# Two transformer blocks on one core: the sums of squares behind two norms as 32-column products, the inverse root on 128x128 values, and a third unit's products spread among them

## The chip, the cores and the metric

One core of a Trainium2 chip runs the whole program. The metric is the device time of one execution in microseconds (us), the median of several runs.

The engines are called by the names of the profile: PE (TensorE, matrix products; PEld is its weight load), DVE (VectorE), ACT (ScalarE), POOL (GpSimd) and SP (SyncE, which issues the weight loads from memory here).

## The reference, cut to what matters

The reference is two transformer blocks on a sequence of 512 tokens with 1024 features. Only a piece of it is touched by the change: twice, a sublayer's output `h` is normed and added to the residual `x`, and the new `x` is normed at once for the next sublayer.

```python
x = x + rmsnorm(h, norm_cross_post[l])               # after the cross attention
h = conv_glu_ffn(rmsnorm(x, norm_ffn_pre[l]), ...)   # first place
x = x + rmsnorm(h, norm_ffn_post[l])                 # after the gated feed-forward
qa, ... = _split(_rmsnorm(x, norm_g) @ w_in, ...)    # second place (second block)

def rmsnorm(x, gain):
    y = x * lax.rsqrt(jnp.mean(x * x, axis=-1, keepdims=True) + RMS_EPS)
    return y * gain
```

The inverse root is one number per token, so a product with the weights can be made before it is known and scaled afterwards.

## The kernel before, in words

**Data.** Activations lie feature-major: eight blocks of 128 features (partitions) by 512 tokens. Weights come as units of 128x1024 values, that is eight 128x128 pieces, one per feature block. Each unit goes through a ring of four slots: SP loads it (L536 to L543), ACT rounds it into a high part (`raise_to`, L1497), POOL subtracts to get the low part (`lower`, L552) and counts `unit_split`. PE then makes three products of 512 columns for each of the eight pieces (high by high, high by low, low by high), 24 in a unit, and counts `unit_done`. DVE reads the finished bank, scales it and counts `emptied`. A slot is loaded again when its unit is done. Every engine works its list in the order in which it is written; PE's waits sit in that list.

**The norm with the work around it.** At both places the DVE function `normed_twice` (L2128) runs over the eight blocks: it scales `h`, adds it to `x`, and makes the low part `xl` of the normed block. ACT's `prepare` (L1500) makes the high part `xh` and the square of each block (L1520, L1527). PE's `early_units` (L679) works beside them. Call the first unit of the next sublayer n0. For each block PE makes four products of n0 and n0+1 with `xh` (L701, L702), then `low_product` of the block before: the sum of squares (`token_sums`, L736) and two products with `xl` (L692). After the eighth block it makes all 24 products of n0+2 and the 24 of n0+3 (`piece`, L617). Between the second and third pieces of n0+2 it calls `spread_tokens` (L755).

**The sum and the inverse root.** `token_sums` takes the squares as the stationary operand and four columns of constants as the moving one, so that 128x4 sums come out, one per token, with tokens on the partitions. After the eighth block ACT takes the root of 128x4 values (L1511), DVE the reciprocal (L2118), and `spread_tokens` turns four columns back into a row of 512 tokens that is the same on every partition. DVE copies it into `rstd` (L2159). From there on DVE can scale n0 and n0+1.

**What follows.** Units n0, n0+1 and n0+2 are split before the norm begins. ACT raises n0+3 in the line after `prepare` (L1956 at the first place, L1971 at the second), so after the root. At the first place the next work is the gated feed-forward: DVE's `gated` (L2598) takes the units in pairs (gate and up), and PE's unit n0+6 goes into the bank of n0+4, so it waits until DVE has read n0+4 (L646). At the second place ACT squares n0 (L1976) before it raises n0+4.

Of the kernel before, what the change touches and what calls it, by code (L numbers as in the profile page):

```python
# [30 lines left out]
P = 128  # L31
# [63 lines left out]

RING = 4


FILL_START, FILL_LEVELS = 1, (0, 1, 2, 3, 4, 5, 6)
W_IN_P = 28  # L100
# [84 lines left out]
def build(nc, x_in, mem_in, w_in, par_in, con_in, moba_in, alibi_in, na_in, dist_in, out):  # L185
    with ExitStack() as ctx:
        def sb(name, shape, dt=F32):
            return ctx.enter_context(nc.sbuf_tensor(name, shape, dt))

        def sem(name):  # L190
            return ctx.enter_context(nc.semaphore(name))
# [33 lines left out]


        head_columns = sb("head_columns", [P, T * HEAD_ROWS])

        arena_r = nc.alloc_sbuf_tensor_at("arena_r", [P, ARENA], F32R, offset=arena_at)

# [156 lines left out]
        def early_bank(n0, n):  # L387

            return score_ps[:, n - n0 - 2, :] if n - n0 in (2, 3) else gemm_ps[:, n % 2, :]
# [63 lines left out]
        square_used = sem("square_used")  # L453
        std_ready = sem("std_ready")
        token_rstd_ready = sem("token_rstd_ready")
        rstd_spread = sem("rstd_spread")
        half_crossed = sem("half_crossed")
        spread_read = sem("spread_read")
# [110 lines left out]
        def _(pe):  # L569
# [47 lines left out]
            def piece(n, o, first, end, h, l):  # L617

                for kt in range(first, end):
                    w = slice(kt * P, (kt + 1) * P)  # L620
                    pe.matmul(o, wh[:, n % RING, w], h[:, kt, :], start=(kt == 0), stop=False)  # L621
                    pe.matmul(o, wh[:, n % RING, w], l[:, kt, :], start=False, stop=False)
                    m = pe.matmul(o, wl[:, n % RING, w], h[:, kt, :], start=False, stop=(kt == KT - 1))  # L623
                if end == KT:
                    m.then_inc(unit_done, 1)
# [53 lines left out]
            def early_units(n0, highs):  # L679


                keep_clock(2)
                pe.wait_ge(unit_split, n0 + 2)
                pe.wait_ge(emptied, n0)
                both = [(n, early_bank(n0, n)) for n in (n0, n0 + 1)]

                def low_product(kt):
                    take(square_ready)
                    token_sums(sq[:, kt % 2, :], kt == 0, kt == KT - 1).then_inc(square_used, 1)
                    pe.wait_ge(rhs_ready, blocks_split[0] + kt + 1)  # L690
                    for n, o in both:
                        m = pe.matmul(o, wh[:, n % RING, kt * P:(kt + 1) * P], xl[:, kt, :], start=False,  # L692
                                      stop=(kt == KT - 1))
                        if kt == KT - 1:
                            m.then_inc(unit_done, 1)

                for kt in range(KT):
                    w = slice(kt * P, (kt + 1) * P)
                    pe.wait_ge(high_made, highs + kt + 1)
                    for n, o in both:  # L700
                        pe.matmul(o, wh[:, n % RING, w], xh[:, kt, :], start=(kt == 0), stop=False)  # L701
                        pe.matmul(o, wl[:, n % RING, w], xh[:, kt, :], start=False, stop=False)  # L702
                    if kt:
                        low_product(kt - 1)
                low_product(KT - 1)
                blocks_split[0] += KT
                for n in (n0 + 2, n0 + 3):
                    pe.wait_ge(unit_split, n + 1)
                    piece(n, early_bank(n0, n), 0, 2, xh, xl)
                    if n == n0 + 2:  # L710
                        spread_tokens()
                    piece(n, early_bank(n0, n), 2, KT, xh, xl)

            def next_unit(n, h, l):

# [20 lines left out]
            def token_sums(squares, first, last):  # L736

                for c in range(T):
                    col = CCOL["col"] + 4 - c
                    m = pe.matmul(turn_ps[:, 0, 0:T], squares[:, c * P:(c + 1) * P], con[:, col:col + T],  # L740
                                  start=(first and c == 0), stop=(last and c == T - 1), skip_group_check=True)
                return m

            def token_norm(apart=1):

# [726 lines left out]
        def _(act):  # L1472
# [24 lines left out]
                    act.activation(wh[:, k % RING, :], raw[:, k % RING, :], ACT.Copy).then_inc(high_split, 1)  # L1497
                    raised[0] += 1

            def prepare(src, gain, h, ready=None, adds=0, tokens=False, banks={}):  # L1500


                base = taken.get(square_added, 0)
                act.activation(eps[:, 3:4], eps[:, 0:1], ACT.Sqrt)
                for b in range(KT):
                    high_and_square(src, gain, h, b, ready, base=base if adds else None, bank=banks.get(b))
                if adds:
                    taken[square_added] = base + adds
                if tokens:
                    take(square_used, 2)  # L1510
                    act.activation(token_std, turn_ps[:, 0, 0:T], ACT.Sqrt, bias=eps[:, 0:1],  # L1511
                                   scale=1.0 / D).then_inc(std_ready, 1)
                else:
                    finish_norm(rstd[:, :])
# [428 lines left out]
            def crossed(b):  # L1943
# [5 lines left out]
                else:  # L1949
# [2 lines left out]
            last = (FIRST["co"] + U_CO - 1) % 2  # L1952
            prepare(y, None, None, crossed, adds=KT - 3, tokens=True,
                    banks={KT - 2: score_ps[:, last, :], KT - 1: gemm_ps[:, last, :]})
            prepare(x, "norm_ffn_pre", xh, lambda b: take(block_ready), tokens=True)
            raise_to(FIRST["fup0"] + 3)  # L1956
            gated()

# [7 lines left out]
                    table_piece(arena[:, (23 + b) * N:(24 + b) * N], alibi_in[:, b * N:(b + 1) * N])  # L1966

            prepare(y, None, None, stored_and_loaded, adds=KT - 2, tokens=True)
            prepare(x, "attn_norm_e_2", xh, lambda b: take(block_ready), tokens=True)
            even, even_out = FIRST["even_in"], FIRST["even_out"]  # L1970
            raise_to(even + 3)  # L1971
            for b in range(5):
# [96 lines left out]
        def _(dve):  # L2069
# [58 lines left out]
            def normed_twice(post, pre):  # L2128


                inverse_tokens()
                added = taken.get(block_ready, 0)
                made = []

                def scale(b):
                    if b >= 2:
                        dve.wait_ge(block_ready, added + b - 1)
                    sent_stt(tmp[:, b % 2, :], y[:, b, :], p_(post, b), spread_rstd, ALU.mult, ALU.mult)
                    made.append(taken[dve_step])

                def accumulate(b):
                    dve.wait_ge(dve_step, made[b])
                    sent(dve.tensor_tensor(x[:, b, :], x[:, b, :], tmp[:, b % 2, :], ALU.add), block_ready)

                scale(0)
                accumulate(0)
                scale(1)
                for b in range(1, KT):
                    if b + 1 < KT:
                        scale(b + 1)  # L2150
                    accumulate(b)
                    low(x, pre, xh, xl, b - 1)
                low(x, pre, xh, xl, KT - 1)
                inverse_spread()

            def inverse_spread():

                inverse_tokens()
                done(dve.tensor_copy(rstd[:, :], spread_rstd))  # L2159
# [803 lines left out]
```

## Time and profile before

| what | value |
|---|---|
| median of 3 runs | 2170.68 us |
| the runs | 2167.75, 2170.68, 2171.09 us |
| the profiled execution, first to last instruction (its span) | 2169.7 us |
| PE busy | 2149.4 us, 99% of the span |
| DVE, POOL, ACT busy | 983.0, 893.9, 847.1 us |
| mean granted clock of PE | 0.997 of full speed |

Of the profiled execution the profile gives the span alone; what lies around it is not listed. In the timelines a line is a group of instructions on one engine: start from the span's start, duration in us, engine, line of the kernel, operation, result<-operands, shape of the (stationary and moving) operands, count, and in brackets the idle time before it with what ended it. Starts are measured; the ends of matrix products are modelled, so the pace of PE is read from start to start.

### The profile page before, as it was taken

What the parts mean: (1) busy time and instruction counts of PE and PEld (TensorE: products, weight loads), DVE (VectorE), ACT (ScalarE), POOL (GpSimd) and SP (SyncE); (2) the same over time, 40 slices, a digit from 0 to 9 for tenths busy, and PEclk for the clock granted to TensorE, in tenths of its full rate; (3) what the DMA queues carried; (4) which work ended last, traced back from release to release, by engine and by line L of the source; (5) the groups of instructions that cost most, each with busy time, mean ns of one, the idle gap of its engine ahead of it and who ended that gap; (6) DMA issues with size and microseconds to landing.
All of it is one profiled execution on the core that took longest, in us unless ns stands there. A gap on an engine that the chain in (4) does not pass through costs nothing.

```text
span 2169.7 us, 27420 instructions
## 1 busy us (share of the span) xinstructions
PE 2149.4 (99%) x10303; PEld 1731.4 (80%) x10303; DVE 983.0 (45%) x1496; ACT 847.1 (39%) x1282; POOL 893.9 (41%) x684
## 2 busy tenths in 40 slices
PE   9999999999999999999999999999999999999999
PEld 7875787788888877767888888888888878888887
DVE  5755645576626143465432231346534655313221
ACT  6435645422222243565433232444333434423221
POOL 5431254154444443213444444433343315444443
PEclk9999999999999999999999999999999999999999
DMA  4222132133322332102222222322222213222223
GB/s 175 78 68 69 57 99 78 59 102 122 106 97 97 110 113 88 50 30 69 97 97 97 97 97 97 106 81 75 78 87 78 72 44 109 97 97 97 97 97 97
DMA packets 55109, 193.24 MB, mean 89 GB/s; under 512 B 6112, under 2 KB 6368, under 8 KB 54752
## 3 DMA queue, kind: packets, MB, share of 16 engines
q1 hardware_dynamic: 50112, 180.41, 25.0%
q10 hardware_dynamic: 4896, 11.41, 1.6%
q8 instruction: 73, 1.20, 0.2%
q14 instruction: 28, 0.23, 0.0%
HBM read 189.69 MB, written 2.10 MB: 88 GB/s over the span
## 4 chain that ended last, share of the span: by engine, by line
issue 52%; POOL 29%; PE 17%; POOLq 1%; DMA 0%; DVE 0%; ACT 0%; SPq 0%; ACTq 0%
POOL wl L552 29%; PE gemm_ps L587 6%; PE gemm_ps L588 6%; PE gemm_ps L589 6%; POOLq L549 0%; POOLq L561 0%; DMA x<-x_in 0%; DVE xl L2090 0%; ACT xh L1892 0%; ACT wh L1497 0%; PE turn_ps L729 0%; DVE x L2236 0%; SPq L526 0%; ACTq L1891 0%
## 5 line engine op out<-in xcount | busy, mean ns | idle before, releaser
L552 POOL TENSOR_TENSOR wl<-raw,wh 128x512 fp32r<-128x512 f32 x678 | 890.1, 1335 | 1258.0 <-ACT wh L1497 1248.8
L1497 ACT ACTIVATE wh<-raw 128x1024 fp32r<-128x1024 f32 x339 | 358.7, 1059 | 752.7 <-DMA raw<-w_in 742.1
L587 PE MATMUL gemm_ps<-xh,wh 128*128 128x512 f32 x1176 | 465.8, 396 | 0.0
L589 PE MATMUL gemm_ps<-xh,wl 128*128 128x512 f32 x1176 | 459.0, 390 | 0.0
L588 PE MATMUL gemm_ps<-xl,wh 128*128 128x512 f32 x1176 | 458.8, 390 | 0.0
L588 PE MATMUL gemm_ps<-arena_r,wh 128*128 128x512 f32 (+1 forms) x1088 | 417.0, 383 | 0.0
L587 PE MATMUL gemm_ps<-arena_r,wh 128*128 128x512 f32 (+1 forms) x832 | 320.0, 385 | 1.2 <-POOL wl L552 0.7
L589 PE MATMUL gemm_ps<-arena_r,wl 128*128 128x512 f32 (+1 forms) x832 | 317.4, 381 | 0.0
L587 PEld LDWEIGHTS gemm_ps<-xh,wh 128*128 128x128 f32 x1176 | 221.5, 188 | 49.6 <-issue 2.3
L588 PEld LDWEIGHTS gemm_ps<-xl,wh 128*128 128x128 f32 x1176 | 221.5, 188 | 47.4 <-issue 2.2
L589 PEld LDWEIGHTS gemm_ps<-xh,wl 128*128 128x128 f32 x1176 | 221.3, 188 | 46.7
L588 PEld LDWEIGHTS gemm_ps<-arena_r,wh 128*128 128x128 f32 x1088 | 205.0, 188 | 41.2 <-issue 1.4
L2090 DVE SCALAR_TENSOR_TENSOR arena<-gemm_ps,rstd 128x512 f32<-128x512 f32 (+1 forms) x116 | 84.7, 731 | 261.9 <-PE gemm_ps L589 211.1
L2236 DVE TENSOR_TENSOR x<-x,gemm_ps 128x512 f32<-128x512 f32 x84 | 57.6, 686 | 316.8 <-PE gemm_ps L589 305.1
L587 PEld LDWEIGHTS gemm_ps<-arena_r,wh 128*128 128x128 f32 x832 | 157.0, 189 | 33.7 <-issue 2.4
L589 PEld LDWEIGHTS gemm_ps<-arena_r,wl 128*128 128x128 f32 x832 | 156.9, 189 | 30.1
L2097 DVE SCALAR_TENSOR_TENSOR tmp<-gemm_ps,rstd 128x512 f32<-128x512 f32 x64 | 44.2, 691 | 207.9 <-PE gemm_ps L589 207.9
L587 PE MATMUL gemm_ps<-y_r,wh 128*128 128x512 f32 x256 | 100.0, 391 | 0.0
L589 PE MATMUL gemm_ps<-y_r,wl 128*128 128x512 f32 x256 | 99.6, 389 | 0.0
L2586 DVE TENSOR_TENSOR arena_r<-sq,arena_r 128x512 fp32r<-128x512 f32 x64 | 93.7, 1464 | 2.2
L621 PE MATMUL gemm_ps<-xh,wh 128*128 128x512 f32 x216 | 88.5, 410 | 1.3 <-DVE xl L2308 0.5
L623 PE MATMUL gemm_ps<-xh,wl 128*128 128x512 f32 x216 | 84.6, 392 | 0.0
(429 smaller groups left out, 2548.6 us busy)
## 6 DMA issues: line engine op xcount, KB each, us to landing
raw<-w_in SPq DMA_DIRECT2D x338, 512.0 KB, 3.4
arena<-na_in ACTq DMA_DIRECT2D x14, 256.0 KB, 2.7
out<-x ACTq DMA_DIRECT2D x8, 256.0 KB, 2.9
x<-x_in SPq DMA_DIRECT2D x6, 256.0 KB, 6.5
arena<-alibi_in ACTq DMA_DIRECT2D x6, 256.0 KB, 3.5
arena<-moba_in ACTq DMA_DIRECT2D x1, 1024.0 KB, 4.8
arena<-mem_in ACTq DMA_DIRECT2D x1, 1024.0 KB, 5.6
arena<-dist_in ACTq DMA_DIRECT2D x1, 896.0 KB, 4.5
```

The source lines that it names most:

```text
L552: m = pool.tensor_tensor(wl[:, k, half], raw[:, k, half], wh[:, k, half].bitcast(F32), ALU.subtract)
L587: pe.matmul(o, wh[:, n % RING, w], h[:, kt, 0:width], start=(kt == 0), stop=False)
L588: pe.matmul(o, wh[:, n % RING, w], l[:, kt, 0:width], start=False, stop=False)
L589: last = pe.matmul(o, wl[:, n % RING, w], h[:, kt, 0:width], start=False, stop=(kt == nkt - 1))
L621: pe.matmul(o, wh[:, n % RING, w], h[:, kt, :], start=(kt == 0), stop=False)
L623: m = pe.matmul(o, wl[:, n % RING, w], h[:, kt, :], start=False, stop=(kt == KT - 1))
L1497: act.activation(wh[:, k % RING, :], raw[:, k % RING, :], ACT.Copy).then_inc(high_split, 1)
L2090: sent(dve.scalar_tensor_tensor(out=o, in0=a, scalar=scalar, in1=b, op0=op0, op1=op1), s)
L2097: done(dve.scalar_tensor_tensor(out=o, in0=a, scalar=scalar, in1=b, op0=op0, op1=op1), s)
L2236: sent(dve.tensor_tensor(x[:, e, :], x[:, e, :], bank(n0, e), ALU.add), emptied)
L2586: done(dve.tensor_tensor(l[:, b, :], sq[:, b % 2, :], h[:, b, :].bitcast(F32), ALU.subtract), rhs_ready)
```

## The change

At the two places, and only there:

- `tile_sums` takes the place of `token_sums`: 32 columns of ones are the stationary operand, the squares of 128 tokens the moving one. Four such products, one for each 128 tokens, go to partitions 0 to 31, 32 to 63, 64 to 95 and 96 to 127 of the same 128 columns.
- The third unit n0+2 follows one block behind n0 and n0+1: after `low_product` of blocks 0 to 4 PE makes the three products of n0+2 with that block. Blocks 5 and 6 come after the last sum.
- Then PE waits for the split of n0+3, calls `spread_tiles`, and makes block 7 of n0+2 and all of n0+3.
- ACT takes the root of 128x128 values and DVE the reciprocal of 128x128 values (each token's value stands on 32 partitions).
- `spread_tiles` makes four products whose stationary operand is one column of the identity, repeated 128 times, and whose moving operand is the 128x128 inverse roots.

The diff, without the new semaphore, the new buffer `tile_rstd` and the constant `TRAILING = 5`:

```diff
 low_product(kt):
-                    token_sums(sq[:, kt % 2, :], kt == 0, kt == KT - 1).then_inc(square_used, 1)
+                    tile_sums(sq[:, kt % 2, :], kt == 0, kt == KT - 1).then_inc(square_used, 1)
 early_units:
                     if kt:
                         low_product(kt - 1)
+                    if kt == 1:
+                        pe.wait_ge(unit_split, n0 + 3)
+                    if 0 < kt <= TRAILING:
+                        piece(n0 + 2, early_bank(n0, n0 + 2), kt - 1, kt, xh, xl)
                 low_product(KT - 1)
                 blocks_split[0] += KT
-                for n in (n0 + 2, n0 + 3):
-                    pe.wait_ge(unit_split, n + 1)
-                    piece(n, early_bank(n0, n), 0, 2, xh, xl)
-                    if n == n0 + 2:
-                        spread_tokens()
-                    piece(n, early_bank(n0, n), 2, KT, xh, xl)
+                piece(n0 + 2, early_bank(n0, n0 + 2), TRAILING, KT - 1, xh, xl)
+                pe.wait_ge(unit_split, n0 + 4)
+                spread_tiles()
+                piece(n0 + 2, early_bank(n0, n0 + 2), KT - 1, KT, xh, xl)
+                piece(n0 + 3, early_bank(n0, n0 + 3), 0, KT, xh, xl)
...
+            def tile_sums(squares, first, last):
+                for c in range(T):
+                    m = pe.matmul(turn_ps[c * HEAD_ROWS:(c + 1) * HEAD_ROWS, 0, 0:P], ones[:, 0:HEAD_ROWS],
+                                  squares[:, c * P:(c + 1) * P], start=first, stop=last)
+                return m
+
+            def spread_tiles():
+                take(tile_rstd_ready)
+                for c in range(T):
+                    row = ident[:, c * HEAD_ROWS:c * HEAD_ROWS + 1].broadcast_to([P, P])
+                    m = pe.matmul(spread_rstd[:, c * P:(c + 1) * P], row, tile_rstd[:, :], start=True, stop=True)
+                m.then_inc(rstd_spread, 1)
 prepare (ACT), with tiles=True at the two places:
-                if tokens:
+                if tiles:
+                    finish_norm(tile_rstd[:, :], P)
+                elif tokens:
 normed_twice (DVE):
-                inverse_spread()
+                take(std_ready)
+                done(dve.reciprocal(tile_rstd[:, :], tile_rstd[:, :]), tile_rstd_ready)
+                take(rstd_spread)
+                done(dve.tensor_copy(rstd[:, :], spread_rstd))
```

`finish_norm` (L1530) waits for all eight sums and takes the root of `turn_ps`, as `prepare` did before with four columns.

## Rows read from the trace of the kernel before

**Rows 1.** The page, part 1: busy us (share of the span) and instructions.

```profile
PE 2149.4 (99%) x10303; PEld 1731.4 (80%) x10303; DVE 983.0 (45%) x1496; ACT 847.1 (39%) x1282; POOL 893.9 (41%) x684
```

**Rows 2.** Timeline of PE, first place (start, duration, as said above).

```profile
412.48 0.95 PE L740 MATMUL turn_ps<-con,sq 128*128 128x4 f32 x8
413.29 0.70 PE L692 MATMUL gemm_ps<-xl,wh 128*128 128x512 f32 x2
413.83 0.40 PE L701 MATMUL gemm_ps<-xh,wh 128*128 128x512 f32 x1
...
427.49 0.95 PE L740 MATMUL turn_ps<-con,sq 128*128 128x4 f32 x8
...
428.86 0.40 PE L621 MATMUL score_ps<-xh,wh 128*128 128x512 f32 x1
...
430.24 0.60 PE L758 MATMUL turn_ps<-con,eps 128*128 128x128 f32 x4
```

**Rows 3.** Timeline of ACT, first place.

```profile
428.48 0.26 ACT L1511 ACTIVATE eps<-turn_ps,eps 128x4 f32<-128x4 f32 x1 [3.00 <-PE turn_ps L740]
428.64 1.05 ACT L1497 ACTIVATE wh<-raw 128x1024 fp32r<-128x1024 f32 x1
```

**Rows 4.** Timeline of POOL, first place.

```profile
429.76 2.53 POOL L552 TENSOR_TENSOR wl<-raw,wh 128x512 fp32r<-128x512 f32 x2 [24.47 <-ACT wh L1497]
```

**Rows 5.** Timeline of DVE, first place: reciprocal, copy, and the read of n0+4.

```profile
428.77 0.18 DVE L2118 RECIPROCAL eps<-eps 128x4 f32<-128x4 f32 x1 [4.19 <-ACT eps L1511]
430.95 0.69 DVE L2159 COPY rstd<-turn_ps 128x512 f32<-128x512 f32 x1 [2.00 <-PE turn_ps L758]
...
450.37 0.69 DVE L2090 SCALAR_TENSOR_TENSOR arena<-gemm_ps,rstd 128x512 f32<-128x512 f32 x1
```

**Rows 6.** Timeline of PE where unit n0+6 begins, first place.

```profile
450.89 0.39 PE L623 MATMUL gemm_ps<-xh,wl 128*128 128x512 f32 x1
451.12 0.50 PE L587 MATMUL gemm_ps<-xh,wh 128*128 128x512 f32 x1
```

**Rows 7.** Timeline of PE: 64-column products in pairs, between products of 128 columns.

```profile
258.75 0.40 PE L1035 MATMUL gemm_ps<-xh,wl 128*128 128x512 f32 x1
259.09 1.09 PE L882 MATMUL out_ps<-sq,arena 128*64 128x128 f32 x16
260.12 0.50 PE L1033 MATMUL gemm_ps<-xh,wh 128*128 128x512 f32 x1
260.45 0.40 PE L1034 MATMUL gemm_ps<-xl,wh 128*128 128x512 f32 x1
```

**Rows 8.** Timeline of PE: 4-column products on two column strips, and full-width ones.

```profile
184.99 1.03 PE L944 MATMUL turn_ps<-arena,con 128*4 128x512 f32 x4
...
406.97 1.88 PE L677 MATMUL out_ps<-con 128*128 128x512 f32 x4
```

**Rows 9.** Durations (ns) by line and by form: a wide reciprocal (DVE), a wide root (ACT).

```profile
L2114 DVE RECIPROCAL arena<-arena x1: 1745/1745/1745, 289.7 to 289.7; 128x256 f32<-128x256 f32 x1
...
L1532 ACT ACTIVATE rstd<-turn_ps,eps 128x512 f32<-128x512 f32 x3 | 2.1, 689 | 11.7 <-PE turn_ps L729 5.9 <-PE turn_ps L723 5.8
```

**Rows 10.** Timelines of ACT, POOL and PE, second place: square of n0, split of n0+4, n0+4.

```profile
807.32 0.63 ACT L1976 ACTIVATE sq<-arena 128x512 f32<-128x512 f32 x1 [2.71 <-DVE arena L2090]
...
808.98 5.04 POOL L552 TENSOR_TENSOR wl<-raw,wh 128x512 fp32r<-128x512 f32 x4 [1.76 <-ACT wh L1497]
...
815.96 0.49 PE L621 MATMUL gemm_ps<-xh,wh 128*128 128x512 f32 x1
```

**Rows 11.** Timeline of PE, before the second place: products at a lower clock.

```profile
780.94 1.11 PE L758 MATMUL turn_ps<-con,eps 128*128 128x128 f32 x4 [0.64 <-DVE eps L2118]
781.85 3.06 PE L677 MATMUL out_ps<-con 128*128 128x512 f32 x4
```

**Rows 12.** Busy us (count) of PE, PEld, DVE, ACT, POOL in a stretch; PEclk, DMA, GB/s.

```profile
780.80:784.20 3.40, 3.26 (x7) 1.92 (x8) 2.09 (x4) 0.53 (x1) 0.21 (x1) 0.50 0.01 2
```

**Rows 13.** Timeline of PE: 32-column transposes, all on the first strip.

```profile
834.09 0.60 PE L664 MATMUL turn_ps<-con,head_columns 128*32 128x128 f32 x4
```

More of the change, by code:

```diff
@@ L96 @@
 RING = 4
+TRAILING = 5
 FILL_START, FILL_LEVELS = 1, (0, 1, 2, 3, 4, 5, 6)
@@ L227, in build @@
         head_columns = sb("head_columns", [P, T * HEAD_ROWS])
+        tile_rstd = sb("tile_rstd", [P, P])
         arena_r = nc.alloc_sbuf_tensor_at("arena_r", [P, ARENA], F32R, offset=arena_at)
@@ L455, in build @@
         token_rstd_ready = sem("token_rstd_ready")
+        tile_rstd_ready = sem("tile_rstd_ready")
         rstd_spread = sem("rstd_spread")
@@ L1498, in raise_to, with prepare @@
                     raised[0] += 1
-            def prepare(src, gain, h, ready=None, adds=0, tokens=False, banks={}):
+            def prepare(src, gain, h, ready=None, adds=0, tokens=False, banks={}, tiles=False):
                 base = taken.get(square_added, 0)
@@ L1954, in _ @@
                     banks={KT - 2: score_ps[:, last, :], KT - 1: gemm_ps[:, last, :]})
-            prepare(x, "norm_ffn_pre", xh, lambda b: take(block_ready), tokens=True)
+            prepare(x, "norm_ffn_pre", xh, lambda b: take(block_ready), tiles=True)
             raise_to(FIRST["fup0"] + 3)
@@ L1968, in _ @@
             prepare(y, None, None, stored_and_loaded, adds=KT - 2, tokens=True)
-            prepare(x, "attn_norm_e_2", xh, lambda b: take(block_ready), tokens=True)
+            prepare(x, "attn_norm_e_2", xh, lambda b: take(block_ready), tiles=True)
             even, even_out = FIRST["even_in"], FIRST["even_out"]
```

## The prediction, before the change was run

> **What bounds the kernel now.** First the page's busy times: PE is busy for 99% of the span, every other engine for under half [rows 1]. So time is won or lost only where PE's own list gets shorter, or where it comes to stand. Next the timeline of PE at the first place. Products of 512 columns follow each other at 0.23 us: six of them fill the stretch from 428.86 to 430.24 [rows 2]. Between two blocks stands the sum of squares, eight records in 0.81 us, and the first product after it takes 0.08 us more than its slot (two products from 413.29 to 413.83) [rows 2]; a sum costs PE 0.89 us. From here PE never stands until the norm is done, since DVE and ACT are ahead of it. Then the timelines of the others, for what must be ready when. After the last sum, begun at 427.49, ACT takes the root at 428.48 and turns to the weights of n0+3 at 428.64 [rows 3]; POOL splits them from 429.76 to 432.29 [rows 4]. The reader is to see that this chain has cover: PE is in unit n0+2 (24 products and the spread) until about 434.8. DVE has its reciprocal at 428.95 and copies the spread root at 430.95 [rows 5]. Last, what DVE's start sets: it reads n0+4 from 450.37 to 451.06 [rows 5], and PE begins n0+6, which needs that bank, at 451.12, one slot of 0.23 us after 450.89 [rows 6]. DVE is just in time there, with 0.06 us to spare. This is the point on which I build.
>
> **The cheaper sums.** No row shows four 32-column products side by side. The nearest shows 64-column products on two strips: 16 records of 128 columns begin after the slot of 258.75 ends (258.98), the next full product begins at 260.12, and the one behind it is 0.33 us later instead of 0.23, so the group costs 1.14 plus 0.1 to 0.11, 1.25 us [rows 7]. One record of 128 columns in single file takes 0.11 us (four in 0.60, of which 0.27 is the last one's length [rows 2]); the 16 are therefore eight steps of two, 0.88 us, and 0.37 us is the way into and out of the narrow form. That two strips run together shows again with four 512-column records in 1.03 us, where full-width ones take 1.88 [rows 8]. The new sum has eight records. Four at a time they are two steps: 1.25 less six steps of 0.11, 0.59 us. Bounds: 0.26 us (the way in and out costs nothing) and 1.25 us (single file, 0.88 plus 0.37). I take 0.59, because rows 7 show both the steps and the way for the same record length. That saves 0.30 us a block, **2.4 us a place**.
>
> The Trainium skill speaks against the change here: "TensorEngine Tiling (Array Packing)", section "Tiling Modes", says that a change of tiling mode drains the engine. The trace agrees (the 0.37 us [rows 7]); by that page's factor of four alone a sum would be 0.22 us.
>
> **The third unit in between.** Its 24 products are the same as before; 15 come earlier. They cost nothing in themselves. The last sum starts later by 15 x 0.23 and earlier by seven cheaper sums: 427.49 + 3.45 - 2.1 = 428.84.
>
> **The wider root and reciprocal.** The root of 128x4 takes 0.26 us [rows 3], of 128x512 0.69 us [rows 9]; 128 columns add about 0.11. The reciprocal of 128x256 takes 1.75 us [rows 9], so half as wide about 0.9 against 0.18 [rows 5].
>
> **The wait for n0+3.** ACT's root began 0.99 us after the last sum's start, 0.29 after its last record [rows 2, 3]. The new sum's last record starts 0.25 us in, so the root begins at 428.84 + 0.54 = 429.38. The rounding of n0+3 follows 0.27 later (0.16 and the 0.11), POOL 1.12 us after that [rows 3, 4], and POOL's 2.53 us end at 433.30. PE has until then 0.59 for the sum and eight products (two of the last block, six of n0+2): it stands before the wait at 428.84 + 0.59 + 1.84 = 431.27. **It waits 2.0 us**, where before the same split lay under n0+2. The reciprocal is done at 429.38 + 0.4 + 0.9 = 430.7, under the same cover; were the wait gone, it would still be in time.
>
> Queued behind the wait are the spread, the last block of n0+2 and n0+3, and DVE waits for the spread.
>
> **The spread.** Four products that were transposes of one record each (0.11 us apart [rows 2]) become four with two records each, as the sums have. Bounds: 0.44 us, as now, and 0.99 us (eight steps and one weight load after the wait). I take 0.99, since other products of this operand type appear in pairs of records [rows 2]: 0.55 us more.
>
> **PE's sum** is -2.4 + 2.0 + 0.55, about +0.2 us a place.
>
> **DVE's sum, first place.** The copy of the root begins 0.38 us after the spread's last record (430.57 to 430.95 [rows 2, 5]): 433.30 + 0.11 + 0.77 + 0.38 = 434.56 instead of 430.95, 3.6 us late. DVE's two pairs of units before n0+4 fill 430.95 to 450.37 [rows 5], 9.7 us each, idle only for ACT's answers, which move along. So n0+4 is read at 454.67 and PE, at its place by 451.3, **waits for 3.3 us**: the place costs 3.5 us, PE's own 0.2 included. Later banks have room: a pair takes DVE 9.7 us and PE 48 products, 11.
>
> **Second place.** The square of n0 and the split of n0+4 move by the same 3.6 us: POOL's first two halves, from 808.98, end at 815.1 instead of 811.5, and PE wants them at 815.96 [rows 10]. Covered with 0.9 us left, so the place costs PE's 0.2. Were that gone too, 3.5 us would come here as well.
>
> SP's load of n0+4 starts with `unit_done` of n0, later by 1.05 us (1.35 for the last sum's start, less 0.30); PE has the wait, the spread and 27 products of n0+2 and n0+3 left before it wants that unit, over 9 us.
>
> **Sum:** 3.5 + 0.2 = +3.7 us. The profiled span is 2169.7, 1.0 below the median of 2170.68; on the median this is **2174.4 us**, +0.17%.
>
> **The rivals.**
>
> A. The sum above, 2173.4 to 2175.4 by its roundings: 0.40.
>
> B. *The stall lowers PE's clock.* Before the second place, after narrow products and an idle gap of 0.64 us, PE's granted clock is 0.50, that is 1.2 GHz instead of 2.4, from 780.80 to 784.20 [rows 11, 12]; four products take 3.06 us there instead of 1.88 [rows 8, 11]. The new stalls of 2.0 and 3.3 us are longer. Such a stretch of 3.4 us does half of its work: +1.7 us when it falls behind the wait at n0+6, 2176.1; two of them 2177.8. Against it: the same narrow sums before the first place left the clock alone (the 1.88 us [rows 8]). This rival is slower beyond what can be told apart: 0.32.
>
> C. *Four strips don't run together.* The 32-column transposes go one after another, four in 0.60 us [rows 13]. In single file a sum costs 0.9 to 1.25 us, up to 0.36 more than now: the sums' 2.4 us saved are lost at each place and DVE is later by as much, from +5.0 to +10.6 over A, 2179 to 2185. Rows 7 and 8 speak against it: 0.08.
>
> D. *The wait for n0+3 costs nothing,* because ACT reaches its weights sooner than I read: then PE saves 1.9 us at the second place, and DVE at the first is 1.6 us late instead of 3.6, 2170.3. The order of ACT's list speaks against it: 0.08.
>
> E. *The way in and out is hidden* under the products around it: a sum costs 0.26 us and both places gain 2.6 us more, 2169.2. Rows 7 speak against it: 0.12. The Trainium skill's page "TensorEngine Tiling (Array Packing)", section "Overview", gives up to four times the speed for 32 columns; no row here shows it for groups this short.
>
> **How the numbers follow.** 0.2%, 4.3 us, is about what a measurement can tell from no change. Slower: B, C and the upper part of A (0.09), 0.49. Faster needs D and E together, about 2165: 0.06 of their 0.20. Within: 0.45. The range leaves out C and most of E: 2170.0 to 2178.0.
>
> **What would show it.** In the changed profile: two starts of the four records of a sum within some 0.03 us, about 0.11 apart, and 0.6 us from the sum's start to the next full pace; idle time of PE before the spread, ended by POOL, of some 2 us at both places; DVE's copy of the root 3 to 4 us later than now, measured from the first block's products; and PE waiting some 3 us for DVE at n0+6 at the first place, nowhere at the second. No wait before the spread, or none at n0+6, makes the prediction wrong, and records of a sum 0.11 us apart one by one make it too low.

## The result and the profile after

The changed kernel takes 2174.56 us against 2170.19 for the kernel before (medians of 20 executions each, taken in turn). The ratio is 1.0023, with a 95% interval of 1.0016 to 1.0029: slower by 3.5 to 6.3 us. The forecast was 2174.4, "slower by over 0.2%" with a chance of 0.49.

The profiled execution has a span of 2171.9 us at a granted clock of 0.996. That is only 2.2 us over before's 2169.7. Two things outside the places hide part of the difference. Ahead of the first place the stretches at half clock (a granted clock of 0.50) lie differently, so that the kernel before reaches the second of the norm's eight blocks 1.3 us later (411.45 against 410.17); and the stages that the change doesn't touch are 1.2 us shorter in this execution of the changed kernel. So the places are compared by themselves, each from the first product of the norm's second block: first place to the first product of n0+6, second place to that of n0+4. Before, these stretches are 39.67 us (411.45 to 451.12) and 29.59 us (786.37 to 815.96).

First the timeline of PE in the changed kernel at the first place: a sum between two blocks, the last sum, and the spread.

```profile
410.86 0.39 PE L706 MATMUL gemm_ps<-xh,wl 128*128 128x512 f32 x1
411.18 0.43 PE L754 MATMUL turn_ps<-sq,con 128*32 128x128 f32 x8
411.54 0.73 PE L696 MATMUL gemm_ps<-xl,wh 128*128 128x512 f32 x2
412.11 0.40 PE L625 MATMUL score_ps<-xh,wh 128*128 128x512 f32 x1
...
427.27 0.43 PE L754 MATMUL turn_ps<-sq,con 128*32 128x128 f32 x8
...
431.71 1.16 PE L763 MATMUL turn_ps<-tile_rstd,con 128*128 128x128 f32 x8 [1.97 <-POOL wl L556]
432.62 0.48 PE L625 MATMUL score_ps<-xh,wh 128*128 128x512 f32 x1
```

These answer to [rows 2]. The sum begins 0.09 us after its slot (410.86 to 411.18 is 0.32, not 0.23), two full products follow it within 0.57 us (411.54 to 412.11) where 0.46 is their own time, and between its start and theirs lie 0.36 us: 0.09 + 0.36 + 0.11, 0.56 us in all, against 0.89 before. The new gap stands ahead of the spread: 1.97 us, ended by POOL.

The timelines of ACT, POOL and DVE beside it, in that order, answer to [rows 3 to 5].

```profile
427.77 0.37 ACT L1556 ACTIVATE tile_rstd<-turn_ps,eps 128x128 f32<-128x128 f32 x1 [2.33 <-PE turn_ps L754]
428.04 1.05 ACT L1519 ACTIVATE wh<-raw 128x1024 fp32r<-128x1024 f32 x1
...
429.16 2.49 POOL L556 TENSOR_TENSOR wl<-raw,wh 128x512 fp32r<-128x512 f32 x2 [26.31 <-ACT wh L1519]
...
428.17 0.95 DVE L2179 RECIPROCAL tile_rstd<-tile_rstd 128x128 f32<-128x128 f32 x1 [3.96 <-ACT tile_rstd L1556]
432.97 0.69 DVE L2181 COPY rstd<-turn_ps 128x512 f32<-128x512 f32 x1 [3.85 <-PE turn_ps L763]
...
452.09 0.69 DVE L2114 SCALAR_TENSOR_TENSOR arena<-gemm_ps,rstd 128x512 f32<-128x512 f32 x1
```

POOL ends the split of n0+3 at 431.65 and the spread begins at 431.71: that chain, not the reciprocal (done at 429.12), sets it. DVE's copy is 22.80 us behind the second block's first product (410.17), where it was 19.50: 3.3 us late. What that lateness does is seen where n0+6 begins (timeline of PE; before it stood there at once, [rows 6]).

```profile
449.49 0.39 PE L627 MATMUL gemm_ps<-xh,wl 128*128 128x512 f32 x1
452.83 0.50 PE L591 MATMUL gemm_ps<-xh,wh 128*128 128x512 f32 x1 [2.95 <-DVE arena L2114]
...
454.34 0.63 PE L591 MATMUL gemm_ps<-xh,wh 128*128 128x512 f32 x1
454.76 0.63 PE L592 MATMUL gemm_ps<-xl,wh 128*128 128x512 f32 x1
```

PE waits 2.95 us for DVE. From 454.34 products come every 0.43 us instead of 0.23. Three windows around it (columns as in [rows 12]):

```profile
449.80:452.80 3.00, 0.08 (x1) 0.00 (x0) 2.91 (x3) 0.00 (x0) 3.00 (x3) 1.00 0.50 172
454.30:457.70 3.40, 3.40 (x9) 2.64 (x8) 2.49 (x4) 1.67 (x2) 0.31 (x1) 0.50 0.00 0
457.80:461.20 3.40, 3.40 (x17) 2.82 (x16) 3.33 (x3) 0.00 (x0) 2.99 (x2) 1.00 0.00 0
```

In the middle one the granted clock is 0.50, that is 1.2 GHz, and 9 products of PE touch it, where 17 touch the next window of the same length. At the second place the spread waits as well, and nothing else does:

```profile
806.47 0.43 PE L754 MATMUL turn_ps<-sq,con 128*32 128x128 f32 x8
...
810.89 1.16 PE L763 MATMUL turn_ps<-tile_rstd,con 128*128 128x128 f32 x8 [1.96 <-POOL wl L556]
```

So the first place is 2.99 us longer (410.17 to 452.83), the second as long as before (789.22 to 818.84, 29.62), and the half clock behind n0+6 adds 1.6 us (n0+6 takes 7.18 us instead of 5.57). Together 4.6 us, against 4.4 between the medians.

### The profile page after: what moved, and what is told of

Read it like the earlier page. It is cut to its first block, busy times and chain, and to the rows that moved or that the text cites. A ratio compares the mean times of both kernels' runs of the same rounds, so it can differ in the third digit from the quotient of the medians.

```text
span 2171.9 us, 27438 instructions
## 1 busy us (share of the span) xinstructions
PE 2146.6 (99%) x10311; PEld 1720.6 (79%) x10311; DVE 986.0 (45%) x1496; ACT 846.9 (39%) x1282; POOL 892.6 (41%) x684
## 4 chain that ended last, share of the span: by engine, by line
issue 53%; POOL 29%; PE 17%; POOLq 1%; ACT 0%; DMA 0%; DVE 0%; SPq 0%; ACTq 0%
POOL wl L556 29%; PE gemm_ps L591 6%; PE gemm_ps L593 6%; PE gemm_ps L592 6%; POOLq L553 0%; POOLq L565 0%; DMA x<-x_in 0%; ACT xh L1916 0%; ACT wh L1519 0%; PE turn_ps L736 0%; DVE x L2263 0%; SPq L530 0%; ACTq L1915 0%
```

## The experiments

Ten kernels, each an edit of the changed kernel, each against the kernel before on the same chip in five rounds. The table sets beside each ratio what its profiled execution shows: how much longer (+) or shorter (-) the two places are than before, and what n0+6 itself took over 5.57 us (half clock at the wait). These are differences of PE's starts in the timelines, in us. In e4, e6 and e7 the second place holds some 1.6 us of a half-clock stretch. One execution of each kernel was profiled, and its time can lie off the median, so the three columns need not add up to the ratio: e2's took 2174.48 us, 5.4 over its median.

| kernel | median | ratio (95%) | place 1 | place 2 | n0+6 |
|---|---|---|---|---|---|
| the change | 2174.56 | 1.0023 (1.0016 to 1.0029) | +3.0 | 0.0 | +1.6 |
| e1 wait behind the spread | 2172.23 | 1.0010 (1.0001 to 1.0020) | +2.0 | -1.5 | +2.7 |
| e2 n0+3 raised early | 2169.08 | 0.9998 (0.9989 to 1.0007) | +2.1 | -2.2 | +2.8 |
| e3 no trailing | 2164.82 | 0.9981 (0.9972 to 0.9990) | -2.2 | -2.3 | 0 |
| e4 stall filled | 2172.72 | 1.0016 (1.0007 to 1.0026) | +3.1 | +1.6 | 0 |
| e5 e3, sums in pairs | 2164.24 | 0.9973 (0.9962 to 0.9984) | -2.3 | -3.0 | 0 |
| e6 old sums, trailing | 2177.19 | 1.0033 (1.0022 to 1.0044) | +5.6 | +3.8 | +1.4 |
| e7 trailing at place 2 only | 2167.34 | 0.9986 (0.9975 to 0.9997) | -1.2 | +1.7 | 0 |
| e8 e2, two blocks trail | 2169.59 | 0.9999 (0.9988 to 1.0010) | +1.0 | -2.2 | +1.6 |
| e9 e5, spread earlier | 2162.88 | 0.9972 (0.9963 to 0.9981) | -3.0 | -3.0 | -0.1 |
| e10 e8, spread earlier | 2167.83 | 0.9987 (0.9976 to 0.9998) | -0.8 | -2.2 | 0 |

**e1: the wait for n0+3 moved behind the spread.**

```diff
-                pe.wait_ge(unit_split, n0 + 4)
                 spread_tiles()
                 piece(n0 + 2, early_bank(n0, n0 + 2), KT - 1, KT, xh, xl)
+                pe.wait_ge(unit_split, n0 + 4)
                 piece(n0 + 3, early_bank(n0, n0 + 3), 0, KT, xh, xl)
```

> PE's wait for the split of n0+3 is moved behind the spread and the last block of n0+2, ahead of n0+3, which alone needs it. Theory (the wait makes DVE late, and DVE's lateness is paid at n0+6): PE stands some 0.4 us before n0+3 at each place instead of 2.0 before the spread; DVE copies the root about 2 us sooner than in the change, 1.2 us later than before; PE waits about 1 us at n0+6 instead of 3.0; the second place gains 1.4 us over the kernel before. Together 2169.5 to 2170.5 us, ratio to the kernel before 0.9995 to 1.0002. Rival (the place of the wait does not matter, the dearer spread and the third unit in between cost the time): 2174 to 2175, ratio 1.002.

Measured: 1.0010, slower than expected. The second place shows the theory: 1.5 us shorter, PE waits only 0.4 behind the spread. The first does not, and three lines of its timelines (PE, DVE, POOL) say why.

```profile
454.04 0.80 PE L591 MATMUL gemm_ps<-xh,wh 128*128 128x512 f32 x1 [3.48 <-DVE arena L2114]
...
435.18 3.42 DVE L2121 SCALAR_TENSOR_TENSOR tmp<-arena,par,tmp 128x512 f32<-128x512 f32 x2
...
435.06 3.00 POOL L556 TENSOR_TENSOR wl<-raw,wh 128x512 fp32r<-128x512 f32 x2 [1.18 <-ACT wh L1519]
```

PE still waits 3.5 us at n0+6. My expectation let the wait before the spread vanish from DVE's path and forgot that PE then comes to n0+6 as much earlier: the stall only shifts. And POOL's split of n0+4 now falls upon DVE's first convolution, which takes 3.42 us for its pair. Before it took 2.45; in the changed kernel it took 1.54, because POOL's split was over by then and held up the step ahead of it instead, 1.13 us against 0.49 here (timelines of DVE, before and changed):

```profile
433.18 2.45 DVE L2097 SCALAR_TENSOR_TENSOR tmp<-arena,par,tmp 128x512 f32<-128x512 f32 x2
...
434.68 1.13 DVE L2418 TENSOR_SCALAR tmp<-arena,par 128x512 f32<-128x512 f32 x1
435.85 1.54 DVE L2121 SCALAR_TENSOR_TENSOR tmp<-arena,par,tmp 128x512 f32<-128x512 f32 x2
```

DVE's copy comes 1.1 us later than before, as expected; with the slow convolution the place becomes 2.0 us longer, and the half clock at the stall adds 2.7, which the expectation did not have.

**e2: ACT raises n0+3 in the middle of `prepare`**, after its fourth block (`n` is n0+3), so that POOL has split it long before.

```diff
+                    if b == 4:
+                        raise_to(n)
```

> The wait stays where the change has it, but ACT raises n0+3 at the fifth block of the norm, so that the split is long done. Theory: no idle time of PE before the spread; DVE copies the root 1.2 us later than in the kernel before; PE waits about 1 us at n0+6; the second place gains 1.9 us. Together 2169.0 to 2170.0 us, ratio 0.9993 to 0.9999. Rival (ACT's 1.05 us of rounding in the norm delays the high parts and PE with them): PE waits for ACT among the blocks, and the ratio stays at 1.001 or above.

Measured: 0.9998, as expected, with no wait ahead of the spread and the second place 2.2 us shorter. But the expected short wait at n0+6 did not come: the waits of PE have it first.

```profile
PE gemm_ps L591 <- DVE arena L2122: 4.5, 2, 4.3
```

So with the wait for n0+3 gone altogether, PE still stands 4.3 us at n0+6. It comes there earlier by the wait that is gone, and DVE is still late: its copy by 1.1 us, as expected, and its first convolution by another 1.1, since POOL's split falls upon it (timeline of DVE):

```profile
435.50 3.54 DVE L2129 SCALAR_TENSOR_TENSOR tmp<-arena,par,tmp 128x512 f32<-128x512 f32 x2
```

What makes the copy late without that wait can be the products put ahead of the spread; e3 takes them away. The 2.8 us of half clock belong to the profiled execution: its places and n0+6 add up to +2.7 us, while the median lies 0.8 us under before's, so the median execution can hardly have held them in full; where it had its half clock is not shown.

**e3: no trailing.** Sums, root, reciprocal and spread as changed, the third unit behind the sums as before.

```diff
-                    if 0 < kt <= TRAILING:
-                        piece(n0 + 2, early_bank(n0, n0 + 2), kt - 1, kt, xh, xl)
...
+                pe.wait_ge(unit_split, n0 + 3)
+                piece(n0 + 2, early_bank(n0, n0 + 2), 0, 2, xh, xl)
                 spread_tiles()
+                piece(n0 + 2, early_bank(n0, n0 + 2), 2, KT, xh, xl)
+                pe.wait_ge(unit_split, n0 + 4)
```

> The narrow sums and the wide spread alone: the third unit's products all stand behind the sums again, with the spread after its second piece, as before the change. Theory: eight sums save 0.3 us each, the spread takes back 0.55, no wait before the spread, DVE copies the root 1 to 2 us sooner than before and PE does not stand at n0+6: 1.9 us gained at each place, 2166.4 us, ratio 0.9980 to 0.9985. Rival (without the third unit PE's block is as short as DVE's, 1.96 against 1.93 us, and PE waits for DVE in the norm): the gain is halved, 2168.3, ratio 0.9990. Rival (the sums save nothing by themselves): 2171, ratio 1.0005.

Measured: 0.9981, faster than both kernels. Timelines of PE and DVE, first place:

```profile
424.98 0.43 PE L751 MATMUL turn_ps<-sq,con 128*32 128x128 f32 x8
...
427.29 1.05 PE L760 MATMUL turn_ps<-tile_rstd,con 128*128 128x128 f32 x8
...
448.60 0.49 PE L591 MATMUL gemm_ps<-xh,wh 128*128 128x512 f32 x1
...
428.44 0.69 DVE L2178 COPY rstd<-turn_ps 128x512 f32<-128x512 f32 x1 [1.62 <-PE turn_ps L760]
```

The copy comes 17.27 us after the second block's first product (411.17), 2.2 earlier than before, and PE goes into n0+6 without a wait. Both places are 2.2 to 2.3 us shorter. Trailing, with the wait it brings, costs the difference to the changed kernel: 5.2 us at the first place and 2.3 at the second, with the half clock on top.

**e4: three products of constants in the stall ahead of n0+6** (`keep_clock(3)`; their results are read by nothing).

```diff
+            keep_clock(3)
             units(fup0 + 6, 2 * FF1_PARTS[0] - 6, xh, xl)
```

> The change with three 512-column products of the identity (2.6 us, results unused) put into PE's list ahead of n0+6, where it stands 3.0 us for DVE. Theory (the stall itself is what costs, the clock adds to it in some executions): PE arrives when DVE is done, as late as before, and its granted clock stays at 1.00 behind n0+6: 2173 to 2174 us, ratio 1.0015, at most 1.4 us under the change. Rival (the loss is the clock's): the loss is gone, ratio 1.000 to 1.0005. Rival (the stall is not the bound): 2.6 us slower than the change, 2177, ratio 1.0035.

Measured: 1.0016. DVE's lateness stays (first place +3.1), the wait at n0+6 is down to 0.36, and the clock there stays at full speed. The 1.8 us to the changed kernel's median fit its 1.6 us of half clock; the two ratios' intervals overlap, so the traces carry this, not the times.

**e5: e3 with the sums of two blocks in one go.**

```diff
+                def pair_of_sums(kt):
+                    for j in (kt - 1, kt):
+                        take(square_ready)
+                        tile_sums(sq[:, j % 2, :], j == 0, j == KT - 1).then_inc(square_used, 1)
...
+                    if kt % 2:
+                        pair_of_sums(kt)
```

> As e3 (no trailing), but PE makes the narrow sums of two blocks in one go, at every second block, so that it goes into and out of the narrow form four times a place instead of eight. Theory: of a sum's 0.57 us some 0.24 are steps and 0.33 the way in and out, so four ways less save 1.3 us a place, 2.6 us in all, and the last sum starts about 1.8 us earlier: DVE's copy of the root moves as much as PE's arrival at n0+6, no wait there. 2162.2 us, ratio 0.9965 to 0.9975; a pair of sums takes 0.8 us from its start to the next full pace. Rival: PE already runs at the pace of the blocks that DVE and ACT deliver (1.92 us against PE's 1.95), so the gain turns into waits for ACT's xh and the time stays at e3's 2164.8, ratio 0.998.

Measured: 0.9973, at the place where it was expected, though not to be told from e3's by the intervals alone. The price of the way is settled by PE's timeline:

```profile
421.58 0.39 PE L709 MATMUL gemm_ps<-xh,wl 128*128 128x512 f32 x1
421.89 0.65 PE L756 MATMUL turn_ps<-sq,con 128*32 128x128 f32 x16
422.47 1.21 PE L699 MATMUL gemm_ps<-xl,wh 128*128 128x512 f32 x4
423.52 0.40 PE L625 MATMUL score_ps<-xh,wh 128*128 128x512 f32 x1
```

A pair costs 0.08 + 0.58 + 0.13, 0.79 us, where two single sums cost 1.12: one way in and out less saves 0.33. The Trainium skill's page "TensorEngine Tiling (Array Packing)", section "Tiling Modes", says that a change of mode drains the engine; a price per change, paid less often here, agrees with it. The second place gains 0.7 us over e3 where 1.3 were expected, and the rival has the rest: two of its blocks start 0.2 us late, each right behind ACT's `xh` of that block, and the product behind each costs 0.1 more. The first of them, timelines of PE and ACT:

```profile
785.95 0.50 PE L708 MATMUL gemm_ps<-xh,wh 128*128 128x512 f32 x1
...
785.17 0.72 ACT L1546 ACTIVATE xh<-x,par 128x512 fp32r<-128x512 f32 x1 [0.68 <-DVE x L2169]
```

The first place gains nothing over e3: one block starts late in the same way (417.26, `xh` done at 417.20), the convolution is hit by POOL's split again (3.52 us), and PE waits 0.91 at n0+6.

**e6: trailing and its wait, with the old sums and spread.**

```diff
-                    tile_sums(sq[:, kt % 2, :], kt == 0, kt == KT - 1).then_inc(square_used, 1)
+                    token_sums(sq[:, kt % 2, :], kt == 0, kt == KT - 1).then_inc(square_used, 1)
...
-                spread_tiles()
+                spread_tokens()
```

> The trailing third unit and the wait for n0+3 ahead of the spread stay, but sums, root, reciprocal and spread are those of the kernel before. Theory: trailing costs the time and the narrow sums win some back. Without them DVE's copy comes 5.6 us late at the first place, which costs 5.6 there, and PE's wait of 2.1 us costs 2.1 at the second: 7.7 us, with the clock's share up to 9.4; 2177.6 to 2179.3 us, ratio 1.0035 to 1.0043. Rival: the wide reciprocal and the two-record spread are what costs, and the old forms under trailing are no slower than the changed kernel, ratio 1.0023 or less.

Measured: 1.0033. First place +5.6, as worked out; second +3.8, of which some 1.7 is half clock. PE's timeline has both stalls:

```profile
435.58 0.65 PE L780 MATMUL turn_ps<-con,eps 128*128 128x128 f32 x4 [1.91 <-POOL wl L556]
...
456.47 0.79 PE L591 MATMUL gemm_ps<-xh,wh 128*128 128x512 f32 x1 [3.21 <-DVE arena L2114]
457.06 0.63 PE L592 MATMUL gemm_ps<-xl,wh 128*128 128x512 f32 x1
```

So it is trailing that costs the time, and the narrow sums win part of it back.

**e7: the change whole at the second place, no trailing at the first.**

```diff
+                trailing = TRAILING if n0 == FIRST["even_in"] else 0
```

> The change stands whole at the second place; at the first the third unit does not trail (as in e3). Theory: trailing costs 5.6 us at the first place, where DVE is just in time for n0+6, and at the second only the wait of 2.0 us before the spread. First place 2.2 us shorter than before, second as before: 2167.6 us, ratio 0.9985 to 0.9995, PE waiting 2.0 us for POOL once and nowhere at n0+6. Rival: trailing costs the same at both places, some 4 us each, and the ratio is 1.000 or more.

Measured: 0.9986, as expected. PE's waits hold one wait for POOL ahead of the spread and a short one at n0+6:

```profile
PE turn_ps L771 <- POOL wl L556: 2.0, 1, 2.0
...
PE gemm_ps L591 <- DVE arena L2122: 0.9, 1, 0.9
```

The first place gained 1.2 us here and not e3's 2.2, with the same instructions. Its copy is as early (17.21 us), but POOL's split started at 432.13, just ahead of DVE's convolution at 432.18, which took 3.48 us; in e3 it started at 430.86, 0.19 behind the convolution's start, and that took 2.44. Timelines of POOL and DVE, e7 and then e3:

```profile
432.13 2.98 POOL L556 TENSOR_TENSOR wl<-raw,wh 128x512 fp32r<-128x512 f32 x2 [1.24 <-ACT wh L1527]
432.18 3.48 DVE L2129 SCALAR_TENSOR_TENSOR tmp<-arena,par,tmp 128x512 f32<-128x512 f32 x2
...
430.86 3.42 POOL L556 TENSOR_TENSOR wl<-raw,wh 128x512 fp32r<-128x512 f32 x2 [1.47 <-ACT wh L1516]
430.67 2.44 DVE L2118 SCALAR_TENSOR_TENSOR tmp<-arena,par,tmp 128x512 f32<-128x512 f32 x2
```

**e8: e2 with two blocks trailing instead of five.**

```diff
-TRAILING = 5
+TRAILING = 2
```

> As e2 (ACT raises n0+3 early, no wait before the spread), but the third unit trails for two blocks instead of five. Theory: every product that goes ahead of the last sum makes DVE's copy later by its own 0.23 us against PE's arrival at n0+6. Six instead of fifteen: PE waits there 1.4 us (2.3 if POOL's split again falls on DVE's convolution) instead of 4.3, the first place is 0.9 us shorter than before (as before in that case), the second 2.2 shorter. 2167 us, ratio 0.998 to 0.999. Rival: the wait at n0+6 is fixed by ACT's and POOL's work on n0+4, not by the products moved, and stays above 3 us: ratio as e2's, 0.9998.

Measured: 0.9999; the wait at n0+6 is 3.0 us. The expectation missed, by its design: the pieces up to block 6 stand ahead of the spread, so that with two blocks trailing fifteen products follow the last sum before the spread (426.21 to 429.65) instead of six. Of the third unit 21 products stand ahead of the spread in e1, e2 and e8 alike, and DVE's copy comes 20.57, 20.57 and 20.67 us after the second block's first product. In e8 that product starts at 410.14, and the timeline of DVE has:

```profile
430.81 0.69 DVE L2189 COPY rstd<-turn_ps 128x512 f32<-128x512 f32 x1 [3.67 <-PE turn_ps L763]
```

It was not how many products go ahead of the last sum, as I had written.

**e10: e8 with the spread six products behind the last sum**, twelve of the unit in all ahead of it.

```diff
-                piece(n0 + 2, early_bank(n0, n0 + 2), TRAILING, KT - 1, xh, xl)
-                pe.wait_ge(unit_split, n0 + 4)
+                piece(n0 + 2, early_bank(n0, n0 + 2), TRAILING, TRAILING + 2, xh, xl)
                 spread_tiles()
-                piece(n0 + 2, early_bank(n0, n0 + 2), KT - 1, KT, xh, xl)
+                piece(n0 + 2, early_bank(n0, n0 + 2), TRAILING + 2, KT, xh, xl)
+                pe.wait_ge(unit_split, n0 + 4)
```

> As e8 (third unit trailing for two blocks, n0+3 raised early), but the spread stands six products behind the last sum, as in e3, instead of fifteen. Theory: e8 missed because its spread stood behind 21 products of the third unit, as many as in e1 and e2; what counts is all of that unit that stands ahead of the spread, before or behind the last sum. Now it is twelve against e3's six, 1.4 us: first place 0.9 us shorter than before (as before if POOL's split falls on DVE's convolution), PE waiting at n0+6 1.4 us (2.3), second place 2.2 shorter: 2167 us, ratio 0.998 to 0.999. Rival: the wait at n0+6 stays at e8's 3.0 us and the ratio at e8's 0.9999.

Measured: 0.9987; first place 0.8 shorter (0.9 expected), second 2.2. The timelines of DVE and PE:

```profile
430.05 0.69 DVE L2189 COPY rstd<-turn_ps 128x512 f32<-128x512 f32 x1 [1.62 <-PE turn_ps L763]
...
450.22 0.50 PE L591 MATMUL gemm_ps<-xh,wh 128*128 128x512 f32 x1 [1.21 <-DVE arena L2122]
```

The copy stands 18.67 us behind the second block's first product, 1.40 behind e3's: six products of 0.23. The corrected rule holds from six products up: with 6, 12 and 21 products of the third unit ahead of the spread (e3, e10, e8) the copy comes 17.27, 18.67 and 20.67 us after the second block's first product. Each costs about its own length at the first place, and nothing at the second.

**e9: e5 with the spread behind three products instead of six.**

```diff
-                piece(n0 + 2, early_bank(n0, n0 + 2), 0, 2, xh, xl)
+                piece(n0 + 2, early_bank(n0, n0 + 2), 0, 1, xh, xl)
                 spread_tiles()
```

> As e5 (sums in pairs, no trailing), with the spread behind three products of the third unit instead of six. In e5's trace the reciprocal was done at 423.96 and the spread began at 424.91, and PE then waited 0.9 us for DVE at n0+6. Theory: what PE does between the last sum and the spread sets DVE's start, and DVE's start sets n0+6. The copy comes 0.7 us earlier, the wait at n0+6 shrinks to some 0.2 us (or stays, if POOL's split of n0+4 again falls on DVE's first convolution and makes it 3.5 us instead of 2.45), the second place stays as in e5. 2163.5 us, ratio 0.9965 to 0.9975. Rival: the spread now waits for the reciprocal and PE stands there instead, ratio as e5's 0.9973 or above.

Measured: 2162.88 us, 0.9972, the lowest time of the study, and below both kernels. Its spread does not wait, nor does n0+6. The lines, of PE and DVE:

```profile
418.97 0.64 PE L756 MATMUL turn_ps<-sq,con 128*32 128x128 f32 x16
...
421.29 1.05 PE L765 MATMUL turn_ps<-tile_rstd,con 128*128 128x128 f32 x8
...
420.08 0.95 DVE L2181 RECIPROCAL tile_rstd<-tile_rstd 128x128 f32<-128x128 f32 x1 [1.84 <-ACT tile_rstd L1558]
422.45 0.69 DVE L2183 COPY rstd<-turn_ps 128x512 f32<-128x512 f32 x1 [1.41 <-PE turn_ps L765]
```

Both places are 3.0 us shorter than before. The copy comes 3.48 us behind the start of the last pair of sums, 0.70 sooner than in e5, as expected. From the second block it is only 0.32 sooner (15.82 against 16.14), for here two blocks of the first place start late behind ACT's `xh` where e5 has one. The convolution took 2.62 us instead of e5's 3.52, so not all of the first place's gain over e5 is the spread's. Against e5 the times alone decide nothing (0.9972 and 0.9973).

## Why the prediction was right, and where it was off

The mechanism was the one forecast, step by step: cheaper sums, a wait for n0+3 that takes most of the gain, DVE late by more than it had to spare, and a stall at n0+6. Its terms against the trace of the changed kernel:

| term | predicted | measured |
|---|---|---|
| a narrow sum | 0.59 | 0.56 |
| last sum, from the second block's products | 1.35 later | 1.06 later (17.10 against 16.04) |
| root, reciprocal | +0.11, 0.9 | +0.11 (0.37), 0.95 |
| wait ahead of the spread | 2.0, both places | 1.97 and 1.96 |
| the spread | 0.99 | 0.99 (0.91 and 0.08 on the next product) |
| DVE's copy | 3.6 late | 3.3 late |
| wait at n0+6 | 3.3 | 2.95 |
| first place | +3.5 | +3.0 |
| second place | +0.2 | 0.0 |
| half clock behind n0+6 | none in the forecast (rival B: +1.7) | +1.6 |

**The sums.** The nearest rows [rows 7] carried: the 64-column group gave both the step and the way, and the new sum came out 0.03 us off. Four records start within 0.02 us (from 411.18) and the next four from 411.31. Rivals C (single file) and E (hidden way) fall; e5 shows the way apart from the steps.

**The waits.** The wait ahead of the spread was right to 0.04 us at both places; from the start of the last sum over ACT's root to the end of POOL's split, 4.46 us were worked out and 4.38 measured (427.27 to 431.65). So rival D falls. The spread took the upper of its two bounds.

**DVE's lateness.** It came out 0.3 us smaller, since the last sum started 0.3 earlier than worked out. DVE's way from the copy to n0+4 was also 0.3 shorter than before (19.12 against 19.42 us), which I had carried over as fixed. It isn't: over all runs it lies between 19.1 and 20.5, by where POOL's split of n0+4 meets the first convolution or the step ahead of it.

**What the 15 earlier products cost.** I charged the first place with the wait for n0+3 and the lateness it brings, and wrote of the products that come earlier: "They cost nothing in themselves." That holds for PE's own list and at the second place, not at the first. e2 takes the wait away and the first place still costs 2.1 us: 21 products of the third unit stand ahead of the spread where six stood, 3.4 us of PE's work that DVE must now wait out, while PE has as much less to do before n0+6. The prediction's sum had this delay, in the 15 x 0.23 by which the last sum starts later, and so it came out right; but naming the wait as the cause was only part of it. By e2 and e3 trailing's own order costs the first place 4.3 us (+2.1 against -2.2): 3.3 by the later copy, 1.0 by POOL's split on DVE's convolution. The wait adds only 0.9 (+3.0 against +2.1): it makes the copy 2.2 us later, but POOL's split is then over before the convolution, and DVE's way to n0+4 is 1.3 shorter (19.12 against 20.45).

**The clock.** I gave the likeliest case no half clock and rival B 0.32. In the profile of the changed kernel the stretch is there, in n0+6, as that rival had it, and the profiles have one at every wait of 2.95 us or more at that point (the change, e1, e2, e6, e8). There is none where the wait is 1.2 us or less (before, e3, e5, e7, e9, e10) nor where it is filled (e4). So this is case A by its steps and rival B by its clock, and the median lies between the two (2174.4 and 2176.1). That it came within 0.2 us of 2174.4 is partly luck: the first place was 0.5 us and the second 0.2 us cheaper than forecast, 1.6 us of half clock were left out, and the kernel before now measured 2170.19 us instead of 2170.68. As a difference, 3.7 us were forecast and 4.4 measured.

**What stays open.** Behind the 2.0 us wait at the second place the profile of the changed kernel shows full clock; those of e4, e6 and e7, with waits of 1.9 to 2.0 us, show half. At the first place the same wait was followed by full clock in all three profiles that have it (the change, e4, e6). I did not find what decides it, and whether other executions of the changed kernel have the stretch at the second place is not shown.

## What to carry to other kernels

Before work is moved into a gap on the busiest engine, ask who waits for what comes after that gap: products that are free for PE's own sum delayed the one small spread that another engine's whole chain hung on, and that engine had 0.06 us to spare. Put what releases others ahead of bulk work in a queue, as early as its inputs allow, and keep the wait for a later unit behind it. A narrow form is worth more when several uses share one way in and out.

## What the runs showed of the hardware

- **Narrow products.** Four 32-column strips do run side by side with 128 moving columns of this type: two steps of 0.11 us for four products. Going into and out of that form costs some 0.33 us each time beside products of full width: 0.34 as 0.56 less two steps, 0.33 by the pairs of e5.
- **POOL against DVE.** DVE's first convolution, a pair with two operands in the on-chip memory, took 1.54 us with POOL idle, and 2.4 to 3.5 us by when POOL's pair of subtractions ran beside it. POOL's pair took 2.5 us (429.16 in the changed kernel) and beside the convolution 3.0 to 3.5. The Trainium skill's page "SBUF — State Buffer", section "Who interferes with whom", says that a DVE instruction with two inputs there contends with a GpSimd instruction that reads there, and that the order of issue decides who blocks; e3 and e7 agree: where POOL starts 0.19 us behind, DVE takes 2.44 and POOL 3.42 us; where it starts 0.05 us ahead, DVE takes 3.48 and POOL 2.98.
- **The clock after a stall.** A wait of 2.95 to 4.3 us at n0+6 came with a granted clock of 0.50, for 3.4 or 6.8 us, in all five profiles that have one; the stretch began between 1.0 us before the wait's end (e1) and 1.5 us behind it (the change), and added 1.4 to 2.8 us to that unit. Where the wait was filled with products (e4) there was none.
